# GpSimd's high half of the weight tiles: a copy in place of a product with one, and one stage barrier taken out twice

## The chip, the cores and the metric

The kernel runs on one core of one Trainium2 chip. The metric is the time of one execution on the device, in microseconds; a time without further words is the median of several runs.

## What is computed

The reference is one inference step of a two-layer decoder trunk for 1024 prompt tokens and 8 sample tokens that share all weights. In float32, with rms norms before each part:

```python
for l in range(2):
    if l == 0:   # retention (4 heads) beside stick-breaking attention (4 heads)
        xp, xs = x + mixer_ab(h, ..., w_in_ab, w_out_ab)
    else:        # a * sigmoid(g), depthwise convolution of width 31, layer norm, silu, product
        xp, xs = x + conformer_conv(h, cv_w1, cv_dw, ..., cv_w2)
    x = x + cross_attn(h, mk, mv, xa_wq[l], xa_wo[l])      # 4 heads of 256 over 256 memory rows
    u = h @ ffn_w_up[l]                                    # 1024 -> 2 x 2816
    gt, val = split(causal_dwconv(u, ffn_dw[l]) + ffn_dwb[l])   # width 3
    x = x + (silu(gt) * val) @ ffn_w_down[l]
```

The outputs are both groups' final norms and the new caches and states.

## The kernel before, in words

All products with weights run on TensorE (PE) with the 1032 tokens as three groups of 344 columns. Weights come as 224 tiles of 128x1024 floats, in the order in which they are used. Each value is split into a high half in fp32r and a low half, the rest, also in fp32r; activations are split in the same way (Hh and Hl, or Gh and Gl in the FFN). A product is then three matmuls: high by high, low activation by high weight, high activation by low weight (`three`, L419 to L425). A tile of 1024 rows is eight chunks, 72 matmuls.

A weight tile t goes through these steps. SP loads it into wraw, slot t % 2, once the tile two before is split (`weight`, L290). POOL (GpSimd) waits for the load and for tile t - 2 to be done on PE (`tile_done`), writes Wh (L393), waits for it, and writes Wl = wraw - Wh (L396); this is `split`, L389 to L397. PE waits for `w_split` and multiplies. In the conformer's convolution ACT writes Wh and DVE writes Wl in POOL's place (tiles 120 to 133); POOL comes back for tile 134. So 210 of the 224 tiles are split by POOL. The second operand of L393 is `one`, one value of 1.0 for each partition, spread over the columns.

The order of work on each engine is written out by hand, with semaphores. In an FFN (PE from L801, DVE from L1618) there are eleven sections of four `up` tiles and two `down` tiles each. PE runs the next section's up tiles, then the down tiles of the section before, in eight pieces n = 0 to 7, alternating between two sets of PSUM banks. DVE empties a set (`ub`, or the addition to X for a down piece, `xadd`, L1624), does the short convolution (`cb`), the gate's product `gf`, and, once ACT has written Gh, the low half Gl = gf - Gh. At the end of a section it writes Gl, then copies a few columns into `tls`, and then does the additions to X of pieces 4 to 7 (`section`, from L1632). PE's piece n + 2 waits for the addition of piece n.

At the end of a product that adds to X, DVE also forms the low half of the new activations and sums their squares in `acc_d` (`add_to_x`, L1274), and PE sums these over partitions (L449). In the conformer DVE does 23 of the 31 taps of the convolution into `ca` (from L1742), and PE the last eight (L850). The mixer's layer starts with stick-breaking attention in four heads (`zs`, `lg`, `sp`, `ea`, `aa`), and goes on with four retention heads, in which DVE also computes the sample tokens' scores with pages of the cache (`junk`, L1437).

Stages end with a barrier. An engine drains and raises its own count, and then waits until all three counts (`end_pe`, `end_dve`, `end_act`) have reached the stage's number:

```python
        def ended(e, n):
            for s in (end_pe, end_dve, end_act):
                e.wait_ge(s, n)

        def end_stage(e, mine, n):
            e.drain().then_inc(mine, 1)
            ended(e, n)
```

In `cross` on PE this barrier is written twice with the same number (L711 and L712), once in each of the two cross-attentions. So from the first cross-attention on `end_pe` is one ahead of the stage's number, and from the second on two ahead; DVE, ACT and SP, which wait for the stage's number, wait for an earlier point of PE. SP's own barriers after that are the ones ahead of the loads of cc (L359) and of us (L374).

Of the kernel before, what the change touches and what calls it, by code (L numbers as in the profile page):

```python
# [26 lines left out]
ALU = mybir.AluOpType  # L27
# [3 lines left out]
P = 128  # L31
# [56 lines left out]
def build(nc, x_in, mem_in, wts, memw, cons, rope, selc, par, stc, stf0, stf1, stret,  # L88
          cache_k, cache_v, cmk, cmv, ptab,
          y, o_sbk, o_sbv, o_retp, o_rets, o_cvp, o_cvs, o_ffn0, o_ffn1, o_st0, o_st1, o_mk, o_mv):  # L90
    with ExitStack() as ctx:
# [12 lines left out]
        def keep(name, shape, dt=F32):  # L104
            return place(name, shape, dt)[0]
# [11 lines left out]
        def sem(name):  # L117
            return ctx.enter_context(nc.semaphore(name))
# [6 lines left out]
        wraw = keep("wraw", [P, 2, 1024])  # L125
        Wh = keep("Wh", [P, 2, 1024], F32R)
# [14 lines left out]
        one = con[:, C_ONE:C_ONE + 1]  # L141
# [70 lines left out]
        w_hi = sem("w_hi")  # L212
# [3 lines left out]
        end_pe, end_dve, end_act = sem("end_pe"), sem("end_dve"), sem("end_act")  # L216
# [6 lines left out]
        def ss(name):  # L223

            if name not in made:
                made[name] = sem(name)
            return made[name]
# [16 lines left out]
# [7 lines that stand above are left out]
# [132 lines left out]
        @block.gpsimd  # L383
        def _(pool):
            for s in set_free:
                pool.sem_inc(s, 1)
            pool.sem_inc(pg_free, 2)

            def split(t, j, landed, first=False):  # L389
                pool.wait_ge(w_raw[j], landed)  # L390
                if not first:
                    pool.wait_ge(tile_done, t - 1)
                pool.tensor_tensor(Wh[:, j, :], wraw[:, j, :], one.broadcast_to((P, 1024)),  # L393
                                   ALU.mult).then_inc(w_hi, 1)
                pool.wait_ge(w_hi, t + 1)
                pool.tensor_tensor(Wl[:, j, :], wraw[:, j, :], Wh[:, j, :].bitcast(F32),  # L396
                                   ALU.subtract).then_inc(w_split, 1)  # L397

            pool.wait_ge(ld_con, 48)
            for j in range(2):  # L400
                split(j, j, 16, first=True)
            for i in range(1, T_W1 // 2 + 1):
                for j in range(2):
                    split(2 * i + j, j, 16 * i + 16)

            pool.wait_ge(w_hi, T_W2)
            pool.wait_ge(w_split, T_W2)
            for i in range(T_W2 // 2, NT // 2):
                for j in range(2):
                    split(2 * i + j, j, 16 * i + 16)  # L410
# [5 lines left out]
        def _(pe):  # L416
# [266 lines left out]
            def cross(l, e0, nk, t0, freed):  # L683
# [16 lines left out]
                for t in range(8, 16):  # L700
# [7 lines left out]
                                     mws[t % 4][:, k * 512:(k + 1) * 512],  # L708
                                     start=(kk == 0 and k == 0), stop=(kk == 3 and k == 1))
                    ins.then_inc(ss("mw_used"), 1)  # L710
                end_stage(pe, end_pe, e0 + 1)  # L711
                end_stage(pe, end_pe, e0 + 1)  # L712

                for c in range(KC):
# [86 lines left out]
            def ffn(l, e1, nk, t0, freed):  # L801
# [28 lines left out]
                end_stage(pe, end_pe, e1)  # L830

            cross(*CR[0])
            ffn(0, E_FF0, 2, T_FFN0, F_FF0)

# [38 lines left out]
            for c in range(KC):  # L873
# [4 lines left out]
                ins.then_inc(ss("l_sqs"), 1)  # L878
            product(T_W2, 4, F_W2, lambda k: pe.wait_ge(ss("l_lo"), k + 1))
            cross(*CR[1])  # L880
            ffn(1, E_FF1, 5, T_FFN1, F_FF1)
            norm_sum(6)
# [1068 lines left out]
```

## Time and profile before

| | |
|---|---|
| three runs | 3602.54, 3602.06, 3598.47 us |
| median | 3602.06 us |
| the profiled execution's own time | 3598.84 us |
| its span, first to last instruction | 3597.1 us |
| mean granted clock of TensorE | 0.957 of full |
| PE busy | 3274.1 us |
| DVE busy | 2020.0 us |
| POOL busy | 952.8 us |
| ACT busy | 726.8 us |

The profile is of one execution. "Busy" is time in which an instruction runs on an engine, and that includes the time in which a started instruction is held up by something else; an instruction that is held shows a longer duration than the same one elsewhere. Idle time is told with what ended it, for example "[0.91 <-DVE X L1224]": 0.91 us until DVE's instruction on X released it. Many instructions are recorded by helpers and so share a line: L1224 is DVE's two-tensor operation, L1228 its three-operand one, L1232 its copy, L896 ACT's activation, L423 PE's matmul in `three`.

### The profile page before, as it was taken

How to read it: one execution, taken by the hardware profiler on the slowest of the kernel's cores; microseconds unless marked ns; L12 is line 12 of the kernel's file. 1: busy time of each engine (PE TensorE's matmuls, PEld its weight loads, DVE VectorE, ACT ScalarE, POOL GpSimd, SP SyncE). 2: the span in 40 equal slices, each digit the busy share in tenths (PEclk: the TensorE clock that was granted, in tenths of full speed). 3: DMA queues.
4: the chain of work that ended last, by engine and by line, in shares of the span. 5: the costliest groups of instructions: out<-in, count | busy, mean ns of one | idle time of the engine just before them, and what ended most of it. 6: DMA issues, size and time to landing. Idle time of an engine off the chain costs nothing. (4 is left out here: it accounts for less than half of the span.)

```text
span 3597.1 us, 45009 instructions
## 1 busy us (share of the span) xinstructions
PE 3274.1 (91%) x19190; PEld 2982.8 (83%) x19190; DVE 2020.0 (56%) x2669; ACT 726.8 (20%) x980; POOL 952.8 (26%) x424
## 2 busy tenths in 40 slices
PE   5999888599969999999997999799969999999996
PEld 4777777499748999999997878499638999999996
DVE  5444555553153656555557899862253656555556
ACT  3655122120121211111112211230121211111111
POOL 2111211034002333333433000033003433333332
PEclk9999988699989999999999999899989999999998
DMA  3011344322332111111112000012342111111111
GB/s 113 31 35 36 130 130 130 113 100 71 106 140 88 51 48 42 48 47 47 42 47 59 30 30 24 25 36 71 106 162 73 46 47 47 48 44 45 47 47 66
DMA packets 83641, 238.15 MB, mean 66 GB/s; under 512 B 15722, under 2 KB 20714, under 8 KB 81522
## 3 DMA queue, kind: packets, MB, share of 16 engines
q1 hardware_dynamic: 74962, 217.96, 18.9%
q10 hardware_dynamic: 8480, 17.32, 1.2%
q8 instruction: 151, 2.47, 0.3%
q14 instruction: 48, 0.39, 0.0%
HBM read 217.93 MB, written 17.32 MB: 65 GB/s over the span
## 5 line engine op out<-in xcount | busy, mean ns | idle before, releaser
L393 POOL TENSOR_TENSOR Wh<-wraw,con 128x1024 fp32r<-128x1024 f32 x210 | 401.3, 1911 | 2578.8 <-PE ps L423 2546.1
L423 PE MATMUL ps<-Hh,Wh 128*128 128x344 f32 x3552 | 792.0, 332 | 53.4 <-DVE Hl L1224 46.2
L423 PE MATMUL ps<-Hl,Wh 128*128 128x344 f32 x3552 | 760.4, 323 | 0.0
L423 PE MATMUL ps<-Hh,Wl 128*128 128x344 f32 x3552 | 755.5, 321 | 0.0
L423 PEld LDWEIGHTS ps<-Hh,Wh 128*128 128x128 f32 x3552 | 606.3, 190 | 88.5 <-issue 71.6
L423 PEld LDWEIGHTS ps<-Hl,Wh 128*128 128x128 f32 x3552 | 607.8, 191 | 0.0
L423 PEld LDWEIGHTS ps<-Hh,Wl 128*128 128x128 f32 x3552 | 597.7, 189 | 0.0
L396 POOL TENSOR_TENSOR Wl<-wraw,Wh 128x1024 fp32r<-128x1024 f32 x210 | 551.4, 2626 | 16.5
L1224 DVE TENSOR_TENSOR X<-ps,X 128x1032 f32<-128x1032 f32 x200 | 244.4, 1230 | 284.0 <-PE ps L423 284.0
L1228 DVE SCALAR_TENSOR_TENSOR cb<-ub,fp,cb 128x1024 f32<-128x1024 f32 x176 | 337.1, 1915 | 93.3 <-ACT cb L896 93.3
L1224 DVE TENSOR_TENSOR ub<-ps,rst_d 128x1032 f32<-128x1032 f32 x88 | 108.5, 1233 | 359.5 <-PE ps L423 191.4
L896 ACT ACTIVATE cb<-ub,fp 128x1032 f32<-128x1032 f32 x88 | 110.2, 1252 | 962.5 <-DVE ub L1224 962.5
L423 PE MATMUL ps<-Gh,Wh 128*128 128x344 f32 x1056 | 225.8, 322 | 18.4 <-DVE X L1224 18.4
L1228 DVE SCALAR_TENSOR_TENSOR ca<-uu,cpar,ca 128x1024 f32<-128x1024 f32 x176 | 233.0, 1324 | 5.6
L423 PE MATMUL ps<-Gl,Wh 128*128 128x344 f32 x1056 | 224.2, 320 | 0.0
L423 PE MATMUL ps<-Gh,Wl 128*128 128x344 f32 x1056 | 224.0, 320 | 0.0
L423 PEld LDWEIGHTS ps<-Gh,Wh 128*128 128x128 f32 x1056 | 176.3, 188 | 24.1 <-DVE X L1224 24.1
L423 PEld LDWEIGHTS ps<-Gl,Wh 128*128 128x128 f32 x1056 | 178.2, 188 | 0.0
L423 PEld LDWEIGHTS ps<-Gh,Wl 128*128 128x128 f32 x1056 | 177.1, 188 | 0.0
L423 PE MATMUL ps<-Hh_s,Wh 128*128 128x344 f32 x768 | 165.8, 325 | 1.3 <-DVEq L249 1.3
L423 PE MATMUL ps<-Hl_s,Wh 128*128 128x344 f32 x768 | 164.0, 322 | 0.0
L423 PE MATMUL ps<-Hh_s,Wl 128*128 128x344 f32 x768 | 163.0, 321 | 0.0
(228 smaller groups left out, 3386.2 us busy)
## 6 DMA issues: line engine op xcount, KB each, us to landing
wraw<-in_wts SPq DMA_DIRECT2D x224, 512.0 KB, 3.6
pg<-in_ck SPq DMA_DIRECT2D x64, 256.0 KB, 2.8
pg<-in_cv SPq DMA_DIRECT2D x64, 256.0 KB, 2.8
cc<-in_cmk SPq DMA_DIRECT2D x16, 1024.0 KB, 7.3
cc<-in_cmv SPq DMA_DIRECT2D x16, 1024.0 KB, 6.0
X<-in_x SPq DMA_DIRECT2D x8, 1032.0 KB, 6.7
mwa<-in_memw SPq DMA_DIRECT2D x16, 512.0 KB, 3.6
mwb<-in_memw SPq DMA_DIRECT2D x16, 512.0 KB, 3.6
```

Source lines behind the costliest of these rows:

```text
L393: pool.tensor_tensor(Wh[:, j, :], wraw[:, j, :], one.broadcast_to((P, 1024)), ALU.mult).then_inc(w_hi, 1)
L396: pool.tensor_tensor(Wl[:, j, :], wraw[:, j, :], Wh[:, j, :].bitcast(F32), ALU.subtract).then_inc(w_split, 1)
L423: ins = mm(o, w[:, wcol[0], wcol[1]:wcol[1] + P], r, start=first and a == 0, stop=last and a == 2)
L896: ins = act.activation(out, in_, f, **kw)
L1224: ins = dve.tensor_tensor(out, a, b, op)
L1228: ins = dve.scalar_tensor_tensor(out=out, in0=in0, scalar=scalar, in1=in1, op0=op0, op1=op1)
```

## The change

POOL writes the high half with a copy (with conversion to fp32r, as the product had) in place of a product with 1.0. And the second of the two equal barriers in PE's part of `cross` is taken out.

```diff
@@ -390,8 +390,7 @@
                 pool.wait_ge(w_raw[j], landed)
                 if not first:
                     pool.wait_ge(tile_done, t - 1)
-                pool.tensor_tensor(Wh[:, j, :], wraw[:, j, :], one.broadcast_to((P, 1024)),
-                                   ALU.mult).then_inc(w_hi, 1)
+                pool.tensor_copy(Wh[:, j, :], wraw[:, j, :]).then_inc(w_hi, 1)
                 pool.wait_ge(w_hi, t + 1)
                 pool.tensor_tensor(Wl[:, j, :], wraw[:, j, :], Wh[:, j, :].bitcast(F32),
                                    ALU.subtract).then_inc(w_split, 1)
@@ -708,7 +707,6 @@
                                      mws[t % 4][:, k * 512:(k + 1) * 512],
                                      start=(kk == 0 and k == 0), stop=(kk == 3 and k == 1))
                     ins.then_inc(ss("mw_used"), 1)
-                end_stage(pe, end_pe, e0 + 1)
                 end_stage(pe, end_pe, e0 + 1)
 
                 for c in range(KC):
```

## Rows read from the trace of the kernel before

**Rows 1.** The page's first part: busy us, share of the span, instructions.
```profile
PE 3274.1 (91%) x19190; PEld 2982.8 (83%) x19190; DVE 2020.0 (56%) x2669; ACT 726.8 (20%) x980; POOL 952.8 (26%) x424
```

**Rows 2.** Waits of POOL: waited for, us in total, times, longest us.
```profile
POOL Wh L393 <- PE ps L423: 2546.1, 207, 281.0
```

**Rows 3.** Waits of PE, same columns.
```profile
PE ps L423 <- DVE X L1224: 18.4, 20, 0.9
...
PE ps L603 <- DVE k L1224: 8.1, 2, 7.5
...
PE ps L850 <- DVE cvo L1224: 5.4, 1, 5.4
...
PE ps L715 <- PEq L249: 4.0, 2, 2.0
...
PE ps L770 <- DVEq L249: 3.0, 2, 1.5
...
PE ps L449 <- DVE acc_d L1224: 1.4, 4, 0.4
```

**Rows 4.** Timeline of POOL, end of an FFN section: start us, us, instruction.
```profile
3184.21 1.90 POOL L393 TENSOR_TENSOR Wh<-wraw,con 128x1024 fp32r<-128x1024 f32 x1 [7.03 <-PE ps L423]
3186.19 3.26 POOL L396 TENSOR_TENSOR Wl<-wraw,Wh 128x1024 fp32r<-128x1024 f32 x1
```

**Rows 5.** Timeline of DVE, the same place.
```profile
3185.25 1.94 DVE L1224 TENSOR_TENSOR Gl<-gf,Gh 128x1032 fp32r<-128x1032 f32 x1
3187.12 2.37 DVE L1232 COPY tls<-ftl 128x40 f32<-128x40 f32 x1
3189.41 2.36 DVE L1224 TENSOR_TENSOR X<-ps,X 128x1032 f32<-128x1032 f32 x2
```

**Rows 6.** Timeline of PE, the same place.
```profile
3190.68 0.59 PE L423 MATMUL ps<-Gh,Wh 128*128 128x344 f32 x2 [0.91 <-DVE X L1224]
```

**Rows 7.** Line L1232: durations in ns (min/median/max), first and last start.
```profile
L1232 DVE COPY tls<-ftl x22: 178/2373/2376, 1248.7 to 3534.3; 128x40 f32<-128x40 f32 x22
...
L1232 DVE CAST selr<-sel x2: 680/682/683, 9.2 to 9.8; 8x1024 fp32r<-8x1024 f32 x2
```

**Rows 8.** Lines L393 and L396, same columns.
```profile
L393 POOL TENSOR_TENSOR Wh<-wraw,con x210: 1892/1895/2875, 18.0 to 3543.9; 128x1024 fp32r<-128x1024 f32 x105
...
L396 POOL TENSOR_TENSOR Wl<-wraw,Wh x210: 2337/2397/3335, 20.0 to 3545.9; 128x1024 fp32r<-128x1024 f32 x105
```

**Rows 9.** Tile acc: the additions and the copy, same columns.
```profile
L1224 DVE TENSOR_TENSOR acc<-acc,sq x7: 1232/1233/3181, 11.3 to 21.1; 128x1032 f32<-128x1032 f32 x7
...
L1232 DVE COPY acc<-sq x1: 698/698/698, 10.5 to 10.5; 128x1032 f32<-128x1032 f32 x1
```

**Rows 10.** Timeline of DVE, start of the first stick-breaking head.
```profile
82.14 0.78 DVE L1224 TENSOR_TENSOR zs<-zs,con 128x128 f32<-128x128 f32 x1
...
83.35 0.29 DVE L1224 TENSOR_TENSOR zs<-zs,con 128x128 f32<-128x128 f32 x1
```

**Rows 11.** Timeline of DVE, first retention head.
```profile
392.42 2.44 DVE L1437 CUSTOM_DVE_ANT_0 junk<-pg,qb 128x128 f32<-128x128 f32 x1
```

**Rows 12.** Timeline of PE, first retention head.
```profile
407.01 2.05 PE L617 MATMUL ps<-vt,kt 128*128 128x128 f32 x16 [1.39 <-DVE kt L1449]
```

**Rows 13.** Timeline of DVE, end of a product that adds to X.
```profile
2804.81 3.43 DVE L1224 TENSOR_TENSOR acc_d<-acc_d,rst_d 128x1032 f32<-128x1032 f32 x1
```

**Rows 14.** Timeline of DVE, end of the first FFN.
```profile
1956.18 5.23 DVE L1224 TENSOR_TENSOR accf<-accf,sqf 128x1032 f32<-128x1032 f32 x2
```

**Rows 15.** Timeline of DVE, the conformer's last two chunks.
```profile
2232.99 36.02 DVE L1228 SCALAR_TENSOR_TENSOR ca<-uu,cpar,ca 128x1024 f32<-128x1024 f32 x22
...
2273.31 29.01 DVE L1228 SCALAR_TENSOR_TENSOR ca<-uu,cpar,ca 128x1024 f32<-128x1024 f32 x22
```

**Rows 16.** Timeline of all engines, the barrier that the change touches.
```profile
970.86 0.34 ACTq L892 DMA_DIRECT2D out_mv<-mv  x1
...
971.76 1.03 PE L715 MATMUL ps<-con,qx 128*8 128x128 f32 x8 [1.99 <-PEq L249]
```

## The prediction

> **What bounds the kernel now.** The page's first part comes first: PE is busy 91% of the span and POOL 26% [rows 1], so POOL's own time is no bound. POOL's waits say the same: before 207 of its 210 high halves it sat idle until PE had finished a tile, 2546 us in all [rows 2]. A shorter high half pays only where POOL holds up somebody else. PE's waits show where something is late: 20 times about 0.9 us for DVE's addition to X in the FFNs, 18.4 us together, ten of them in each FFN, and several smaller ones [rows 3].
>
> One such gap, read on three engines. POOL starts Wh at 3184.21 and Wl at 3186.19 [rows 4]. DVE's Gl starts at 3185.25 and takes 1.94 us; the 128x40 copy to tls after it takes 2.37 us, until 3189.49, which is where Wl ends (3189.45); then come two additions to X, and PE resumes at 3190.68 after 0.91 us idle [rows 4 to 6]. Of the 22 copies to tls the shortest takes 178 ns and the median 2373 [rows 7]: the copy waits until POOL's instruction is done. Gl, which reads two SBUF tiles, waits too: an undisturbed addition of such tiles takes 1.23 [rows 9]. And it goes both ways: this Wl takes 3.26 us where the shortest takes 2.34 [rows 4, 8], because Gl ran first. In order: Gl ends 1.08 us after Wh (3187.19 against 3186.11), Wl 2.26 us after Gl, tls with Wl, then X.
>
> **The price of the copy.** No row has a POOL instruction with one input on 1024 columns. The product with the broadcast one takes 1895 ns (median), the difference of two tiles 2397 [rows 8]. The nearest pair on one engine is DVE's: adding two SBUF tiles 1232 ns, copying the same 1032 columns 698 [rows 9], a ratio of 0.566. I take 1895 x 0.566 = **1.07 us**, 0.82 less than the product. The lower end is DVE's copy itself, 0.70; the upper end is POOL's dearer operation, 2.39, so a loss is not excluded. I stay near the ratio because POOL's time already depends on what its second operand is, by a quarter, and the copy has none.
>
> The Trainium skill's GPSIMD Engine Reference, section "Engine selection", says that operations with one input run at roughly line rate on that engine and those with two about half as fast as on the Vector engine; with the 1.03 cycles per element of its section "Elementwise" at 1.2 GHz the copy would be an estimated 0.88 us, and the sum below about 21 us all the same, as Wl then goes ahead of Gl. The same section gives about 1.8 cycles per element as the best case of a tight loop, which speaks against so large a saving; the first rival is the case that comes nearest to it.
>
> **The FFN sections.** With Wh at 1.07 us it ends at 3185.28, just as Gl begins. Gl then runs undisturbed, 1.24 us, to 3186.49; Wl ends 2.26 us later, at 3188.75, and tls and X follow 0.70 us earlier than now. Should Wl get in ahead of Gl (Wh under some 0.96 us), it ends near 3187.6, Gl 1.08 later, tls costs its 0.18 and X starts some 0.65 earlier: the order hardly matters. Both are less than the 0.91 us that PE waits, so all of it reaches PE. PE's later products in the section then come earlier by as much, and with them the tiles for which POOL and DVE wait. 20 x 0.70 = **14.0 us**.
>
> **Other places where POOL is on the path**, each by the 0.82 us that Wh loses unless something caps it:
> - Start: of the seven additions to acc the longest takes 3.18 us instead of 1.23 [rows 9], beside POOL's first splits, and PE's first column sums wait for the last. One saving, 0.8.
> - First stick-breaking head: zs takes 0.78 us, the next one 0.29 [rows 10], and PE waits for it. 0.4. The same delay later in the heads finds PE at work on other tiles and counts nothing.
> - First retention head: a junk of 128x128 takes 2.44 us behind Wl [rows 11], the next ones and kt come after it, and PE's L617 waits 1.39 for kt [rows 12]; L603 just before waits 0.6 for k [rows 3]. Together 1.2. In the next two heads PE has no such wait.
> - Products into X ahead of cross-attention and FFN, four of them: acc_d takes 3.43 us behind Wl [rows 13], and PE's L449 waits 0.35 for it, 1.4 over the four [rows 3], which is the cap. 1.4.
> - End of the first FFN: two accf take 5.23 us instead of twice 1.23 [rows 14], and PE's column sums wait; 0.6, since an accf may start ahead of Wl as Gl does.
> - Conformer: 22 products take 36.02 us with two splits beside them, 29.01 without [rows 15], and PE's L850 waits 5.4 for DVE [rows 3]. Two savings, 1.7.
>
> These are 6.1 us.
>
> **The removed line.** It takes a second drain of PE and a second barrier out of each cross-attention. ACT has issued its last store there at 971.20, and PE resumes at 971.76 [rows 16]; the second barrier is somewhere in these 0.56 us. I take 0.25 for each of the two, 0.5, with 0 and 1.1 as ends. What it adds: end_pe no longer runs one ahead (two after the second cross-attention), so DVE, ACT and SP wait for PE's own count of a stage. That is free where DVE's or ACT's last instruction uses PE's last product: at the barrier after the attention it is DVE for which PE waits, at L770 [rows 3], and SP, with the loads of cc queued behind that barrier, waits for the same DVE. At the conformer's end DVE waits for PE's last column sum in any case, now for the drain behind it as well; ACT's two stores queue behind that drain and its squares behind the stores, but the squares need DVE's first subtraction too. At most 0.2 us, taken as nothing.
>
> What a faster Wh starts earlier: Wl, hence SP's load of the next raw tile, by 0.8 us; POOL waits for PE after that load anyway [rows 2], so no transfer becomes late.
>
> **Total.** 14.0 + 6.1 + 0.5 = 20.6. The profiled execution took 3598.84 us (its span 3597.1 and 1.7 around it), 3.2 under the median of the three runs, 3602.06. Against that execution the sum gives 3578; against the median, which I forecast, **3581 us**. With 0.70 for the copy the sections gain some 0.86 each, 17, and the others some 7.5, 25 in all: 3577, and 3 less for the spread of the runs.
>
> **Rivals.**
> 1. The copy is bound by its loop and not by its reads, and saves half as much, at 1.48 us. Then Gl still waits for Wh, the sections gain 0.41 each, 8.2, the other places 3, with the line 11.7: 3590. For it: POOL's two operations have two inputs each and differ by a quarter, so reads are not all. By the skill's 1.8 cycles per element the price would be an estimated 1.54 us and the time 3592. Chance 0.10.
> 2. The copy takes as long as the product, 1.9 us. Then only the line counts: 3601.6, which is no change. For it: the broadcast operand is one value for each partition, so it may cost next to nothing now. Chance 0.10.
> 3. Slower: rounding to fp32r in a copy goes a dearer way than in arithmetic. Above 1.90 us the addition to X starts later by the excess in each of the 20 sections, and nothing covers it, since PE stands waiting there. At the subtraction's 2.39 that is 20 x 0.5 = 10 and 4.5 elsewhere, less the line: 3616. It decides from 1.90 and can be measured from about 2.2. Against it: DVE's conversion to fp32r of 1024 columns takes 682 ns, no more than its plain copy [rows 7, 9], and both of POOL's products write fp32r now. Chance 0.08.
>
> **How the numbers follow.** The forecast has 0.72. A measurement of this kernel can tell about 0.2%, 7.2 us, from no change. Faster by more: the forecast and most of rival 1, 0.80. Within it: rival 2 and the rest of rival 1, 0.12. Slower: 0.08. The range takes the forecast's own bounds, 3574 to 3585, and reaches over rival 1 to 3597, which leaves out 0.18.
>
> **What would show it.** The row of L393 gives the price: about 1.07 us. PE's wait for DVE's X should fall from 18.4 us to about 4; Gl at a section's end should take about 1.24, or, if Wl goes first, tls about 0.18. The conformer's slow 22 products should come down from 36.0 to about 34.3, L449's four waits vanish, L715's shorten by some 0.25 each. If L393 is near 1 us and PE still waits 0.9 us in each section, the reading of the gap is wrong; if L393 stays near 1.9 or rises, the price was.

## The result, and the profile after

The changed kernel takes **3571.08 us** (median of six runs, 3569.03 to 3575.33), the kernel before 3600.26 beside it (six runs, 3598.02 to 3602.54). The ratio is 0.9921, interval 0.9908 to 0.9934. The forecast was 3581 in a range from 3574 to 3597: the direction is right, the size 8 us short, and the time lies 3 us under the range. The profiled execution took 3570.55 us (span 3568.8) against 3598.84 before, 28.3 less.

The page's first part after the change, to hold against [rows 1]:

```profile
PE 3265.9 (92%) x19190; PEld 2977.9 (83%) x19190; DVE 1894.6 (53%) x2669; ACT 726.7 (20%) x980; POOL 776.1 (22%) x424
```

POOL is busy 177 us less, 210 tiles by about 0.84. DVE is busy 125 us less with the same 2669 instructions, none of which the change touches: all of it is gained by instructions that ran beside one of POOL's in the kernel before. PE has the same 19190 matmuls and shows 8.2 us less busy time; this will matter below.

The two rows of POOL after (durations min/median/max in ns), which answer to [rows 8]:

```profile
L393 POOL CAST Wh<-wraw x210: 1036/1042/2035, 17.7 to 3515.8; 128x1024 fp32r<-128x1024 f32 x105
...
L395 POOL TENSOR_TENSOR Wl<-wraw,Wh x210: 2339/2407/3487, 18.8 to 3516.9; 128x1024 fp32r<-128x1024 f32 x105
```

The copy costs 1042 ns where 1.07 us was forecast; the difference that follows it is unchanged.

PE's waits after (waited for: us in total, times, longest), against [rows 3]:

```profile
PE ps L422 <- DVE X L1222: 4.0, 20, 0.2
...
PE ps L848 <- DVE cvo L1222: 3.7, 1, 3.7
PE ps L713 <- ACTq L249: 3.5, 2, 1.8
```

The twenty waits for DVE's X fell from 18.4 us to 4.0, as forecast. The conformer's fell from 5.4 to 3.7, those at the attention's start from 4.0 to 3.5, and the four for acc_d are gone.

One FFN section after the change, the one of [rows 4 to 6], on POOL, then DVE, then PE (start us, us, instruction, idle before it):

```profile
3160.38 1.04 POOL L393 CAST Wh<-wraw 128x1024 fp32r<-128x1024 f32 x1 [7.89 <-PE ps L422]
3161.50 3.41 POOL L395 TENSOR_TENSOR Wl<-wraw,Wh 128x1024 fp32r<-128x1024 f32 x1
```

```profile
3161.43 1.22 DVE L1222 TENSOR_TENSOR Gl<-gf,Gh 128x1032 fp32r<-128x1032 f32 x1
3162.57 2.38 DVE L1230 COPY tls<-ftl 128x40 f32<-128x40 f32 x1
3164.87 2.36 DVE L1222 TENSOR_TENSOR X<-ps,X 128x1032 f32<-128x1032 f32 x2
```

```profile
3166.14 0.74 PE L422 MATMUL ps<-Gh,Wh 128*128 128x344 f32 x3 [0.20 <-DVE X L1222]
```

The order is the one forecast: the copy ends at 3161.42, Gl starts at 3161.43 and runs undisturbed in 1.22 us (1.94 before), Wl goes behind it, the copy to tls still lasts as long as Wl, and X follows. PE's wait is 0.20 us instead of 0.91.

**Where the 28.3 us came from.** Both kernels issue the same matmuls in the same order, so the start of each can be compared one by one. What PE is earlier by, and where that grew:

| place | forecast | measured |
|---|---|---|
| start, to PE's first matmul | 0.8 | 1.2 |
| stick-breaking heads, 47 to 346 us | 0.4 | 3.4 (from 1.3 to 4.7) |
| retention | 1.2 | 1.4 |
| the four L449 | 1.4 | 2.4 (0.61, 0.62, 0.54, 0.61) |
| 20 FFN sections | 14.0 | 14.3 (10.18 to 17.32, and 21.00 to 28.14) |
| end of the first FFN | 0.6 | 0.7 |
| conformer | 1.7 | 1.7 |
| start of the two cross-attentions | 0.5 | 0.4 |
| clock of TensorE from L738 on, at 1033 and 2644 us | none | 3.4 (1.7 and 1.7) |
| sum | 20.6 | 28.9 |

The sum is 0.6 us over the measured 28.3; the difference is many small steps both ways. The 0.4 at the start of the cross-attentions is all that the trace shows at the removed line's own place; the experiments show that it is not all that this line is worth.

### The profile page after: what moved, and what is told of

The parts are those of the page before. It is cut to its first block, busy times and chain, and to the rows that moved or that the text cites. A ratio compares the mean times of both kernels' runs of the same rounds, so it can differ in the third digit from the quotient of the medians.

```text
span 3568.8 us, 45005 instructions
## 1 busy us (share of the span) xinstructions
PE 3265.9 (92%) x19190; PEld 2977.9 (83%) x19190; DVE 1894.6 (53%) x2669; ACT 726.7 (20%) x980; POOL 776.1 (22%) x424
## 3 DMA queue, kind: packets, MB, share of 16 engines
q10 hardware_dynamic: 8480, 17.32, 1.3%
HBM read 217.93 MB, written 17.32 MB: 66 GB/s over the span
## 4 chain that ended last, share of the span: by engine, by line
PE 84%; DVE 11%; DMA 2%; ACT 1%; issue 1%; SPq 0%; DVEq 0%; ACTq 0%
PE ps L422 68%; PE ps L848 3%; PE ps L750 2%; PE ps L695 2%; PE ps L706 2%; PE ps L724 1%; DVE tls L1230 1%; DVE junk L1590 1%; DVE X L1222 1%; PE ps L543 1%; PE ps L530 1%; PE ps L534 1%; PE ps L485 1%; PE ps L520 1%; DVE ca L1226 1%
## 5 line engine op out<-in xcount | busy, mean ns | idle before, releaser
L393 POOL CAST Wh<-wraw 128x1024 fp32r<-128x1024 f32 x210 | 221.5, 1055 | 2726.2 <-PE ps L422 2693.9
L1226 DVE SCALAR_TENSOR_TENSOR cb<-ub,fp,cb 128x1024 f32<-128x1024 f32 x176 | 276.0, 1568 | 93.3 <-ACT cb L894 93.3
```

Source lines behind the costliest of these rows:

```text
L393: pool.tensor_copy(Wh[:, j, :], wraw[:, j, :]).then_inc(w_hi, 1)
L1226: ins = dve.scalar_tensor_tensor(out=out, in0=in0, scalar=scalar, in1=in1, op0=op0, op1=op1)
```

## The experiments

Three sets of runs, each with the kernel before beside it on the same chip (medians 3600.08, 3600.62 and 3601.36 us).

### The two parts of the change, each by itself

The copy with the second barrier kept:

```diff
-                pool.tensor_tensor(Wh[:, j, :], wraw[:, j, :], one.broadcast_to((P, 1024)),
-                                   ALU.mult).then_inc(w_hi, 1)
+                pool.tensor_copy(Wh[:, j, :], wraw[:, j, :]).then_inc(w_hi, 1)
```

> The copy is in, PE's second barrier stays. My theory: nearly all of the 28 us come from the copy, and the removed line is worth what PE's L715 shows, about 0.2 us in each of two places: 3571.5 us against 3571 with both edits. The rival: the 8 us by which the forecast fell short come from the removed line (the engines wait for another point of PE from the first cross-attention on): then about 3579.

Measured: 3579.61 us (3576.09 to 3580.74), ratio 0.9944 (0.993 to 0.9958). That is 20.5 us faster than before, and 8.5 slower than with the line out as well.

The product kept, the second barrier out:

```diff
-                end_stage(pe, end_pe, e0 + 1)
                 end_stage(pe, end_pe, e0 + 1)
```

> PE's second barrier is out, the product with one stays. My theory: 0.4 us faster than the kernel before, 3600 us, which can't be told from no change; in the trace PE's wait at L715 falls from 1.99 to about 1.77 and nothing else moves. The rival as in copy_alone: about 3592.

Measured: 3598.26 us (11 runs, 3592.54 to 3600.84), ratio 0.9996 (0.9987 to 1.0005), no difference that can be told. So the two parts don't add: the copy gives 20.5, the line about 2 by the medians (4.7 at the end of the interval), both together 29. Beside the copy the line is worth some 9 us. The trace gives the line 0.4 in idle time; the other 8 had to be found.

### The copy to tls, put behind two additions to X

This moves the small copy that POOL's Wl holds up to a place where Wl is done. It was to show whether the reading of the section's end is right.

```diff
+                    for n in (4, 5):
+                        between(n)
                     dve.wait_ge(*of_layer(l, "f_ft", 4 * i + 4))
...
-                    for n in range(4, 8):
+                    for n in (6, 7):
                         between(n)
```

On the kernel before:

> The kernel before, with one step of DVE moved: the copy to tls at the end of an FFN section comes after the additions of pieces 4 and 5 to X, not ahead of them. My theory: PE's 0.91 us in each of the 20 sections are there because that copy waits for POOL's Wl and the addition stands behind it; then the 18.4 us of PE waits for X go to about 0 and the time to some 3582 us, with the product still in. The rival: the addition to X waits for POOL itself, or is late because of Gl: then PE waits 0.5 us or more in each section and the time stays above 3590.

Measured: 3575.72 us (3574.37 to 3579.35), ratio 0.9934 (0.992 to 0.9948), 24 us faster where less was expected. On the changed kernel:

> The changed kernel with the same move of the tls copy. My theory: it takes the remaining 0.2 us of PE's wait in each of 20 sections, 4 us, so 3567 us; against tls_after_product the copy is then worth only what it brings outside the sections, 11 to 15 us. The rival: the copy helps the sections in a way that has nothing to do with tls, so its gain adds to the move's in full: about 3553.

Measured: **3561.88 us** (3560.51 to 3563.51), ratio 0.9895 (0.988 to 0.991). This is the fastest kernel of the study, 9.2 us faster than the changed one. The line of the copy to tls, in the changed kernel, in the first and in the second of these two:

```profile
L1230 DVE COPY tls<-ftl x22: 175/2374/2383, 1237.6 to 3506.1; 128x40 f32<-128x40 f32 x22
```

```profile
L1232 DVE COPY tls<-ftl x22: 174/175/179, 1250.3 to 3520.9; 128x40 f32<-128x40 f32 x22
```

```profile
L1230 DVE COPY tls<-ftl x22: 173/175/178, 1239.2 to 3504.8; 128x40 f32<-128x40 f32 x22
```

So 128x40 floats cost 2.37 us or 0.175, by whether POOL's Wl had started first. The Trainium skill's SBUF — State Buffer, section "Who interferes with whom", says that the engine that comes first holds the shared port pair for its whole instruction and that issue order decides who is blocked; these three lines agree.

Both gains are larger than PE's wait row promised. On the kernel before, PE's start moved 1.17 us per section, 23.3 in all, where [rows 3] has 18.4. The same wait shows in the row of PE's weight loads, before and after the change:

```profile
PEld ps L423 <- DVE X L1224: 24.1, 20, 1.2
```

```profile
PEld ps L422 <- DVE X L1222: 9.7, 20, 0.5
```

24.1 answers to the 23.3 and 9.7 to the 9.2. The wait of the weight loads was the better measure here; the matmuls' row had a quarter less before and less than half after.

With tls out of the way the change is worth 13.8 us (3575.72 less 3561.88), and without that 29. In the sections it is then worth nothing: from PE's first matmul behind the additions at one section's end to the same matmul nine sections later, PE needs 624.75 us in the kernel before (1301.48 to 1926.23), 618.33 in the changed kernel, and 614.26 with the move in both (1302.04 to 1916.30 with the product, 1291.77 to 1906.02 with the copy). All that the change gained in the sections was part of a stall that a reordering takes away whole. Of the 13.8, the profiles put some 5 to TensorE's clock, the subject of the next part: there are three stretches at half clock near the cross-attentions with the product, none with the copy.

### TensorE's clock behind the attention's start

The profile of the copy alone differs from that of the changed kernel at four places near the cross-attentions. PE's timeline at the first one, the copy alone, then the changed kernel:

```profile
965.78 1.69 PE L714 MATMUL ps<-con,qx 128*8 128x128 f32 x8 [1.99 <-PEq L249]
967.26 7.92 PE L725 MATMUL ps<-mkT,qx 128*128 128x256 f32 x31
```

```profile
964.63 1.03 PE L713 MATMUL ps<-con,qx 128*8 128x128 f32 x8 [1.77 <-ACTq L249]
965.50 7.07 PE L724 MATMUL ps<-mkT,qx 128*128 128x256 f32 x32
```

The same eight matmuls take 1.69 us instead of 1.03. The stretches from there, the copy alone (window, its length, then busy us of PE, PEld, DVE, ACT and POOL, the granted clock, DMA share, GB/s):

```profile
966.00:969.40 3.40, 3.40 (x14) 2.54 (x12) 1.09 (x2) 1.79 (x3) 0.00 (x0) 0.50 0.99 410
969.40:972.80 3.40, 3.40 (x17) 3.01 (x16) 1.00 (x2) 0.55 (x1) 0.00 (x0) 1.00 0.07 29
```

The granted clock is 0.50 here, 1.2 GHz, and back at 2.4 behind it; the changed kernel has 2.4 GHz here. There are four such stretches that the changed kernel does not have, at 966.0, 1027.4, 2570.3 and 2631.7 us: behind PE's start of the attention and behind the first matmuls on L737 that follow an idle time of 2.76 us, in both layers. By the start of the same matmuls they cost 1.7 us each, 6.7 of the 7.9 between the two profiled executions. If this is the cause, two matmuls that fill PE's time ahead of the barrier should bring the time back without taking the barrier out. So both kernels ran again, plain and filled (the extra product of `ones` goes to a PSUM bank that the stage then overwrites):

```diff
+                for _ in range(2):
+                    mm(ps[:, 0, :], ones, con[:, 0:512], start=True, stop=True)
                 end_stage(pe, end_pe, e0 + 1)
```

The changed kernel as it is:

> The changed kernel again, beside copy_alone on the same chip, for a second profile of each. Theory A (clock): what the removed line is worth beyond its 0.4 us is TensorE's clock in the cross-attention. With one barrier PE's idle time at the stage's start is 1.77 us and the granted clock stays at its upper level there; so no stretch at half clock near 965 or 2567 us in this profile either, and 3570 to 3574 us. Theory B (chance): the low stretches come and go from one execution to the next whatever the kernel; then they can stand here too, and the two kernels' medians come within 3 us of each other.

Measured: 3570.56 us (3569.08 to 3572.39), ratio 0.9915 (0.9902 to 0.9929), with 2.4 GHz at all four places.

The copy alone as it is:

> The copy with the second barrier kept, again. Theory A: 1.99 us idle at the start of the attention stage, the clock at half behind it in most executions, 3577 to 3581 us, 6 to 9 above after_again. Theory B: within 3 us of after_again.

Measured: 3579.81 us (3575.78 to 3582.64), ratio 0.9942 (0.9928 to 0.9956), with 1.2 GHz again at the four places (963.6, 1025.0, 2567.8 and 2629.3).

The changed kernel, filled:

> The changed kernel with two matmuls of 128x512 more on PE, just ahead of its barrier at the end of the stage with the memory's products, in a PSUM bank that is free there; nobody reads what they write. They take about 0.9 us in which PE would wait for ACT. Theory A: the clock stays up there already, so nothing changes: within 2 us of after_again. Theory B: the same, since the low stretches have no cause there.

Measured: 3572.75 us (3570.28 to 3574.72), ratio 0.992 (0.9906 to 0.9933): nothing to gain there.

The copy alone, filled:

> copy_alone with the same two matmuls ahead of its two barriers. Theory A: PE's idle time there falls from 1.99 to about 1.1 us, the clock stays up behind it, and most of the 6 to 9 us between copy_alone and the changed kernel go away: within 3 us of after_filled. Theory C (the extra drain and the counts themselves cost the time, not the clock): it stays 6 to 9 us slower than after_filled.

Measured: 3570.91 us (3569.72 to 3575.77), ratio 0.9922 (0.9909 to 0.9936). With both barriers in place it is as fast as the changed kernel, 8.9 us faster than without the filling; there is 2.4 GHz at the four places, and PE's wait at the barrier, 4.0 us over the two before [rows 3], is 0.5 us at each, where some 1.1 was expected:

```profile
PE ps L716 <- PEq L249: 0.9, 2, 0.5
```

This settles where the 9 us are. What the second barrier costs beside the copy is for the most part not its own time but TensorE's clock, behind the idle time that it lengthens from 1.77 to 1.99 us and again later. That the fillers sit only at the barrier and the second stretch, 60 us later, goes too, shows that the two hang together; how is not shown. Nor does idle time alone decide: the changed kernel idles 2.75 us at L736 and stays at 2.4 GHz, and the kernel before idles the same 1.99 us at its barriers [rows 3]. One profile has both outcomes, the kernel before with the copy to tls moved, in its first and in its second layer:

```profile
972.44 1.57 PE L715 MATMUL ps<-con,qx 128*8 128x128 f32 x8 [1.99 <-PEq L249]
```

```profile
2574.38 1.03 PE L715 MATMUL ps<-con,qx 128*8 128x128 f32 x8 [1.99 <-PEq L249]
```

Over all the profiles the clock fell behind 1.99 us there in five places of eight, behind 1.77 us in none of fourteen, and behind the later 2.75 us in thirteen of twenty-eight. Does the kernel before pay there too? The same filling in it:

> The kernel before with the two matmuls ahead of its two barriers. Theory A (clock): the kernel before pays the clock in part of its executions only; its profile shows two stretches at half clock, both behind L738 and none behind L715. 3593 to 3599 us: between the 2 us that taking the barrier out gave and the 9 us that the matmuls gave to copy_alone. Theory C: no change, 3600 us.

Measured: 3598.24 us (11 runs, 3596.97 to 3603.25), ratio 0.9996 (0.9987 to 1.0005), no difference that can be told. Its profile, like that of the kernel before, has one stretch of 1.2 GHz in each layer, none of them at the attention's start, and the fillers leave them. In the kernel before the first is this one (columns as above):

```profile
1033.00:1036.40 3.40, 3.40 (x6) 1.30 (x4) 0.50 (x1) 1.00 (x2) 0.00 (x0) 0.51 0.00 0
```

It begins 1.4 us after the same idle time of 2.75 us (PE resumes at 1031.68); in the kernel before's second layer, and in the copy alone, the clock falls as PE resumes, and in the changed kernel not at all. So near the cross-attentions the kernel before loses 3.4 us in two such stretches, the copy alone 6.7 in four, and the changed kernel none. One barrier by itself does not ensure that: the product with one barrier still has one such stretch, at 2638 us. So taking the line out took one stretch away beside the product, which with its 0.4 makes the 2 us measured, and four beside the copy. Why it is these is not shown.

### What holds PE in the stick-breaking heads

Two readings of the larger gain there: that every later split in the heads delays DVE, and DVE PE, or that it comes from elsewhere. DVE's sp at 177 us, before and after the change:

```profile
177.14 1.99 DVE L1228 SCALAR_TENSOR_TENSOR sp<-zs,lg 128x512 f32<-128x512 f32 x1
```

```profile
174.22 1.10 DVE L1226 SCALAR_TENSOR_TENSOR sp<-zs,lg 128x512 f32<-128x512 f32 x1
```

And PE beside it, before and after:

```profile
178.64 0.64 PE L423 MATMUL ps<-Hh,Wl 128*128 128x344 f32 x3
179.19 1.13 PE L531 MATMUL ps<-sp,con 128*128 128x512 f32 x2
180.15 1.02 PE L535 MATMUL ps<-rr,con 128*128 128x512 f32 x2
```

```profile
175.72 0.64 PE L422 MATMUL ps<-Hh,Wl 128*128 128x344 f32 x3
176.20 1.02 PE L530 MATMUL ps<-sp,con 128*128 128x512 f32 x2
177.06 1.02 PE L534 MATMUL ps<-rr,con 128*128 128x512 f32 x2
```

Before, sp takes 1.99 us, after, 1.10, since POOL's Wl beside it is done sooner. From the start of the group ahead to that of L535 PE needs 1.51 us (178.64 to 180.15) and after the change 1.34 (175.72 to 177.06): 0.17 us in this place, with no idle time shown in either kernel. The matmuls start a little late, and the waiting is counted as PE's busy time. The product back in for the tiles of the heads alone:

```diff
+                if 2 <= t < T_RET + 5:
+                    pool.tensor_tensor(Wh[:, j, :], wraw[:, j, :], one.broadcast_to((P, 1024)),
+                                       ALU.mult).then_inc(w_hi, 1)
+                else:
+                    pool.tensor_copy(Wh[:, j, :], wraw[:, j, :]).then_inc(w_hi, 1)
```

> The changed kernel with the product with one for the 15 tiles that POOL splits in the stick-breaking heads, the copy for the others. From the two traces, those heads became 3.4 us shorter in the changed kernel, where the forecast had 0.4. Theory L (PE waits for sp in short pieces which the profile counts as busy matmuls): PE's L530 comes later by steps of 0.3 to 0.5 us again, 3.4 us in all, 3574.5 us. Theory N (the heads are shorter for another reason, such as the clock behind PE's first wait): the step at 363 us is under 1.5 us.

Measured: 3575.66 us (3572.17 to 3576.67), ratio 0.9927 (0.9913 to 0.9941), against 0.9915 and 0.9921 for the changed kernel: some 4 us slower, at the edge of what the intervals tell. The starts of the matmuls are plainer: against the changed kernel PE falls behind in steps of 0.3 to 0.5 us at L530 and once at L520, 3.0 us by 341 us. The fifteen products are those of

```profile
L394 POOL TENSOR_TENSOR Wh<-wraw,con x15: 1893/1895/1898, 58.8 to 357.3; 128x1024 fp32r<-128x1024 f32 x15
```

So the heads' gain is made in the heads, split by split, and is the copy's.

### Other prices for the high half

An operation with two SBUF inputs that are both the raw tile, instead of the copy (Wh is then twice the weight, and Wl its negative):

```diff
-                pool.tensor_copy(Wh[:, j, :], wraw[:, j, :]).then_inc(w_hi, 1)
+                pool.tensor_tensor(Wh[:, j, :], wraw[:, j, :], wraw[:, j, :], ALU.add).then_inc(w_hi, 1)
```

> The changed kernel, with wraw + wraw in place of the copy: an operation of POOL with two tiles as inputs (the weights' high half is twice the value then, so the outputs are others). It should take about 2.35 us as Wl's difference does. Theory L (what counts is how long POOL's instruction holds DVE): 0.45 us dearer than the product, 9 us in the 20 sections and about 5.7 elsewhere: 3613 us, slower than the kernel before. Theory I (what counts is that the copy reads one input and leaves DVE a path): like the product, 3598 us.

Measured: 3596.44 us (10 runs, 3592.8 to 3600.23), ratio 0.9991 (0.9981 to 1.0), that is, like the product with the barrier out (0.9996). The price that this run was made for did not come:

```profile
L393 POOL TENSOR_TENSOR Wh<-wraw x210: 1892/1894/2876, 17.8 to 3537.9; 128x1024 fp32r<-128x1024 f32 x105
```

1894 ns, the product's 1895, and not the difference's 2397 [rows 8]. So the run gives no point above the product's price, and cannot tell whether DVE is held by the length of POOL's instruction or by its having two inputs. The changed kernel's own trace can, where a two-input instruction of DVE starts under POOL's copy (DVE, then POOL):

```profile
385.27 1.12 DVE L1435 CUSTOM_DVE_ANT_0 junk<-pg,qb 128x128 f32<-128x128 f32 x1
386.32 0.08 DVE L1435 DVE_READ_ACCUMULATOR2_ANT zz<- 128x1 f32 x1
386.32 0.28 DVE L1435 CUSTOM_DVE_ANT_0 junk<-pg,qb 128x128 f32<-128x128 f32 x1
```

```profile
384.55 1.69 POOL L393 CAST Wh<-wraw 128x1024 fp32r<-128x1024 f32 x1 [9.13 <-PE ps L422]
```

The first junk takes 1.12 us where the next takes 0.28, and ends 0.15 us behind the copy (386.39 against 386.24). So the copy, with one input, holds DVE until it is done; it is cheaper for DVE because it is shorter. What the sum does show is that a whole second SBUF operand costs POOL no more than one value spread over the columns when it is the same tile; whether the difference is dearer for its two tiles or for its operation was not tried.

Half a copy, 512 of the 1024 columns (the other half of Wh is set to zero once, so the high half of those columns is left out of every product):

```diff
+            pool.memset(Wh[:, :, 512:1024].bitcast(F32), 0.0).then_inc(ss("half"), 1)
+            pool.wait_ge(ss("half"), 1)
...
-                pool.tensor_copy(Wh[:, j, :], wraw[:, j, :]).then_inc(w_hi, 1)
+                pool.tensor_copy(Wh[:, j, 0:512], wraw[:, j, 0:512]).then_inc(w_hi, 1)
```

> The changed kernel, with the copy of 512 of the 1024 columns alone (the other half of Wh stays zero, so the weights' rounding is another there). About 0.57 us. Theory L: Wl now starts ahead of Gl, ends near 3187.25 on the clock of the gap read before, Gl 1.08 later, X 1.0 us earlier than in the kernel before: 0.3 more than the copy for each section, 6 in all, and as much elsewhere: 3559 us. Theory O (with Wl ahead, Gl pays what Wl gains): nothing more in the sections, 3565 us.

Measured: 3568.76 us (3566.49 to 3573.64), ratio 0.9915 (0.9899 to 0.9931), only 2 us under the changed kernel. The copy costs 0.43 us less:

```profile
L395 POOL CAST Wh<-wraw x210: 609/613/1610, 17.8 to 3512.1; 128x512 fp32r<-128x512 f32 x105
```

```profile
L1232 DVE COPY tls<-ftl x22: 171/172/179, 1238.9 to 3504.6; 128x40 f32<-128x40 f32 x22
```

Now Wl starts ahead of Gl, and the copy to tls is free, the other order that the prediction's second case describes. PE is 0.29 us earlier per section than in the changed kernel, 5.7 in all, as expected for the sections. Elsewhere it loses: by 404 us PE is 2.3 us behind the changed kernel, with steps of 0.85 us at L520 and 1.59 at L623, because other pairs of POOL's and DVE's instructions changed order (a copy of 128x8 to qsel, now behind Wl, takes 2.10 us instead of 0.17, kms 3.22 instead of 1.62). A stretch at half clock at 2623 us, which the changed kernel does not have, takes 1.7 more. The expectation that the rest would gain as much failed.

## Why the prediction was right in direction and short in size

**The price** held: 1.07 us from the ratio of DVE's two rows, 1.04 measured. With it rivals 1 to 3 fell at once, each of which needed 1.48 us or more. The reason given for the ratio, that POOL's time depends on what its second operand is, is not borne out: the sum of a tile with itself took the product's time. So the ratio came out right without its argument. The Trainium skill's GPSIMD Engine Reference has a line rate for one input in its section "Engine selection" and 1.03 cycles per element in "Elementwise"; the estimate of 0.88 us from these was nearer than the 1.54 us from the best case of a tight loop in the same section. The two lengths measured, 1042 ns for 1024 columns and 613 for 512, give 0.84 ns a column and some 0.18 us beside that.

**The sections** held in mechanism, order and size: 0.71 us each against 0.70. So did the conformer, retention and the first FFN's end. The sections' wait fell as forecast, though the row it was read from understates it (18.4 against 24.1 in the weight loads' row); since 0.71 was less than either gives for a section (0.9 and 1.2), nothing capped it.

**The step that failed first** is "the removed line ... I take 0.25 for each of the two, 0.5, with 0 and 1.1 as ends". As idle time it was right: 0.2 each. What was left out is what PE's clock does after the idle time. Beside the copy the line is worth some 9 us, shown by taking it away and by filling the idle time in its place; beside the product, about 2. And the copy alone, forecast at 20.1, came out at 20.5 by two errors that cancel: 25 us by its own places, and 3.4 from two half-clock stretches of the kernel before, less 6.7 that four cost now (small steps make up the rest). The forecast's agreement with the copy alone is therefore luck, and no proof of its terms.

**The second** is "the same delay later in the heads finds PE at work on other tiles and counts nothing". It counts 3.0 us. The view shows PE at work without a gap, because waits of some tenths of a microsecond show as late starts inside a run of matmuls. PE's busy time, 8.2 us lower with the same matmuls, holds such waits and the time at the half clock: it fell by 2.9 us in the heads and by 3.4 in the two stretches.

**The third** is a cap: the four L449 were held to PE's wait of 1.4 in [rows 3], and gave 2.4.

**The base** is the last: 3581 stood on a median of three runs, 3602.06; six runs gave 3600.26, so 1.8 of the 9.9 us between forecast and result are the base. The terms of the table make the other 8.1, to 0.2: heads 3.0, clock 3.4, L449 1.0, the rest 0.9.

**What stays open:** what besides the length of the idle time decides whether the clock falls, and so why the kernel before, with the same idle times of 1.99 and 2.75 us as the copy alone, keeps 2.4 GHz behind the first; and what makes POOL's difference dearer than its sum of one tile.

## What to carry to other kernels

An engine far from being the bound (POOL, 26%) can be worth some 25 us through what its instructions hold up on a neighbour: price each place by the instruction that is held, and try first whether the held instruction can stand elsewhere, since moving one copy of 40 columns gained 24 us alone and 9 more on top of this change, and left the change nothing to gain in the sections. Don't take PE's idle rows as a cap on what an earlier release can give; read the weight loads' waits too, and after a change compare the start of the same matmuls. And where a change shortens or lengthens an idle time of PE, look at the granted clock behind it, and, if it is half, fill the idle time with matmuls before anything is rebuilt: that gave 9 us beside the copy, and nothing to be told beside the product.

## What was not expected of the hardware

- In the copy alone, half of TensorE's clock for 3.4 us after a barrier, with 1.7 us lost each time, where the idle time ahead was longer by only 0.2 us than in the changed kernel; filled with two 512-column matmuls, the loss was gone at the barrier and also 60 us later. The same 1.99 us left the clock at 2.4 GHz in other profiles.
- A copy of 128x40 floats on DVE that lasts 2.37 us because POOL's subtraction started first, against 0.175 with none beside it.
- POOL's sum of a tile with itself at 1894 ns, the price of the product with one broadcast value, where the difference of two tiles takes 2397.
